# Routing of a mixture of experts: an own index test for the first gather, rows scaled by TensorE, slot weights moved into the first step

## The reference

```python
x = x + g1 * (jnp.concatenate([attn, rec], axis=-1) @ lp['w_out'])
h2 = modulate(rms_norm(x, lp['norm2']), sh2, sc2)
x = x + g2 * moe(h2, ...)
# moe: top-1 of 4 groups, then top-2 of the 8 experts in it
p_grp = softmax(x32 @ wg + bg); g_sel = argmax(p_grp)
top_v, top_i = lax.top_k(fine_sel, 2)
w_fine = softmax(top_v) * p_sel
act = silu(hg) * hu * combine;  y = einsum(act, w_down)
```

## Time and profile before

| | us |
|---|---|
| median of 3 runs | 623.18 (621.56 to 624.5) |
| the profiled execution's own time | 622.47 |
| its span, first to last instruction | 620.6 |
| TensorE busy | 584.6 (94%) |
| DVE / ACT / POOL busy | 350.2 / 179.7 / 101.7 |
| chain that ended last: TensorE / transfers / DVE | 73% / 15% / 5% |
| mean granted clock of TensorE | 0.991 |

### The profile page before, as it was taken

How to read it: one execution, slowest core, us unless ns; L and a number is a source line. 1 busy time by engine, 2 the same in 40 slices (tenths; PEclk the granted TensorE clock), 3 DMA queues, 4 the chain that set the end, 5 groups by cost and what they waited for, 6 DMA issues and landing times.

```text
span 620.6 us, 9361 instructions
## 1 busy us (share of the span) xinstructions
PE 584.6 (94%) x3274; PEld 325.4 (52%) x3275; DVE 350.2 (56%) x777; ACT 179.7 (29%) x375; POOL 101.7 (16%) x134
## 2 busy tenths in 40 slices
PE   5989999999998999999999889999999999987995
PEld 2544455555565677645555446555555555444542
DVE  2746898655565887654666883334342433341357
ACT  4203887701145777731111101111111111111110
POOL 4000011121261000000000111122212222221122
PEclk9999999999999999999999999999999999997998
DMA  8999833430039638539114959999999999999995
GB/s 320 378 370 361 337 124 147 175 136 2 0 85 270 265 101 265 236 126 383 68 69 143 379 175 384 420 419 417 419 417 416 417 420 420 421 417 418 412 403 224
DMA packets 48674, 176.21 MB, mean 284 GB/s; under 512 B 11540, under 2 KB 18592, under 8 KB 34944
## 3 DMA queue, kind: packets, MB, share of 16 engines
q1 hardware_dynamic: 36992, 154.86, 63.9%
q0 software_dynamic: 6688, 15.48, 7.2%
q10 hardware_dynamic: 4960, 5.42, 2.5%
HBM read 163.37 MB, written 21.14 MB: 297 GB/s over the span
## 4 chain that ended last, share of the span: by engine, by line
PE 73%; DMA 15%; DVE 5%; SPq 4%; issue 2%; ACTq 1%; DVEq 0%; ACT 0%; POOL 0%; POOLq 0%
PE ps L1802 18%; PE ps L1617 11%; PE ps L1542 8%; PE ps L1818 8%; PE ps L1530 7%; DMA expert_w<-exp_w_up 5%; PE ps L1657 4%; PE ps L1684 4%; DMA gate_w<-lru_wx 3%; PE ps L1666 3%; DMA w_mod_ring<-w_mod 2%; PE ps L1505 2%; SPq L369 2%; PE ps L1770 2%; PE ps L1451 2%; DMA recurrence<-w_mod 2%
## 5 line engine op out<-in xcount | busy, mean ns | idle before, releaser
L1802 PE MATMUL ps<-expert_w,hT_mixT 128*64 128x256 f32 x1120 | 135.6, 392 | 7.8 <-DMA expert_w<-exp_w_up 7.4
L1802 PEld LDWEIGHTS ps<-expert_w,hT_mixT 128*64 128x64 f32 x1120 | 84.5, 136 | 62.6 <-issue 19.1
L1530 PE MATMUL ps<-hT_mixT,w 128*128 128x128 f32 (+1 forms) x256 | 72.6, 437 | 1.2 <-DVE hT_mixT L954 1.2
L1617 PE MATMUL ps<-w,hT_mixT 128*128 128x512 f32 x160 | 71.9, 597 | 0.0
L1818 PE MATMUL ps<-expert_w,w 128*64 128x512 f32 x280 | 65.8, 598 | 0.0
L770 ACT ACTIVATE w<-ps 128x128 f32<-128x128 f32 x36 | 10.0, 277 | 188.4 <-PE ps L1802 188.4
L1530 PEld LDWEIGHTS ps<-hT_mixT,w 128*128 128x128 f32 x256 | 38.9, 191 | 35.8 <-issue 32.7
L1349 DVE SCALAR_TENSOR_TENSOR w<-w,ps 128x128 f32<-128x128 f32 x36 | 10.3, 287 | 81.2 <-ACT w L770 81.2
L1542 PE MATMUL ps<-w_qkv,hT_mixT 128*128 128x512 f32 (+1 forms) x160 | 53.1, 488 | 0.0
L1367 DVE TENSOR_TENSOR w<-ps,w 128x1024 f32<-128x1024 f32 x17 | 20.8, 1225 | 56.6 <-PE ps L1818 56.6
L1617 PEld LDWEIGHTS ps<-w,hT_mixT 128*128 128x128 f32 x160 | 29.1, 191 | 29.9 <-issue 29.7
(11 more groups left out here) (293 smaller groups left out, 759.5 us busy)
## 6 DMA issues: line engine op xcount, KB each, us to landing
expert_w<-exp_w_down SPq DMA_DIRECT2D x31, 1024.0 KB, 18.2
expert_w<-exp_w_gate SPq DMA_DIRECT2D x29, 1024.0 KB
expert_w<-exp_w_up SPq DMA_DIRECT2D x29, 1024.0 KB
w_mod_ring<-w_mod SPq DMA_DIRECT2D x14, 1024.0 KB, 6.5
y_rows<-zero_rows POOLq DMA_DIRECT2D x10, 512.0 KB, 9.4
expert_w<-y_rows SPq DMA_DIRECT2D x10, 512.0 KB, 9.8
recurrence<-w_mod SPq DMA_DIRECT2D x8, 512.0 KB, 9.7
w<-w_in SPq DMA_DIRECT2D x4, 1024.0 KB, 17.0
```

Source lines behind the costliest of these rows:

```text
L1530: ins = pe.matmul(ps[:, bank, 0:n], w1v[:, c, m * P:(m + 1) * P], HM[:, c, lo:lo + n], start=(c == 0), stop=(c == DC - 1))
L1617: ins = pe.matmul(ps[:, 2 * (t % 2) + half, :], HM[:, c, t * P:(t + 1) * P], w1v[:, c, half * 512:(half + 1) * 512], start=(c == 0), stop= ...
L1802: ins = pe.matmul(ps[r, 2 + k, 0:2 * P].rearrange("p (k f) -> p k f", k=2), xT[:, c, r], gate_up(i)[:, :, c, k:FF:FC], start=(c == 0), sto ...
```

## The change

Five things are done, all around the routing of the last tile.

1. **Index of the first gather.** In step 0 are the tokens of pair 0 in block 0. DVE makes `slots` of the last tile first, then `hit0` = (block number is 0) x (pair is 0), without the sums over pairs; ten matmuls with one column give the tokens, and DVE writes them into idxc, which the first gather uses. `hit`, its matmuls and `tid` follow.
2. **Rows of the last tile.** DVE doesn't make h2 of the last tile any more. ACT makes `diag`, the identity times the rows' factors, TensorE adds ident x shift2 and diag x scaled rows in banks 2 and 3, and ACT evicts them and writes them out.
3. **Logits of the last tile** are split: chunks 0 to 3 ahead of the last transposes.
4. **Slot weights.** The matmuls stand within the first expert step, behind its first half; `step1w` and `firsts` are made after `x_out(0)`.
5. **Smaller moves.** The g2 rows are issued after h2, the logits and `rank` of the last tile; the fillers are fewer and shorter; two semaphores of turns become one.

The names `fore` and `aft` are chunks 0 to 3 and 4 to 7.

```diff
+        hit0 = W1[:, 584:584 + TOP * NT // 2].bitcast(F16).rearrange("p (t k) -> p t k", t=NT)
...
+        diag = HM[:, 7, P:2 * P]
...
-            for i, v in enumerate((1, 0)):
-                sp.dma_start(g2[:, i, :], a["mod_rows"][v, 5 * D:6 * D].partition_broadcast(P)).then_inc(S["g2_in"], 16)
             sp.dma_start(kept_down[0], wd_v[KEPT, :, 0:D].rearrange("p (c n) -> p c n", c=DC)).then_inc(kept_in, 16)
             sp.wait_ge(S["h2"], NT)
             sp.wait_ge(S["lg_mm"], NT)
+            sp.wait_ge(S["rank_mm"], NT)
+            for i, v in enumerate((1, 0)):
+                sp.dma_start(g2[:, i, :], a["mod_rows"][v, 5 * D:6 * D].partition_broadcast(P)).then_inc(S["g2_in"], 16)
             sp.wait_ge(S["xg_in"], 16)
             sp.dma_start(ring[:, HOME[5], 0:EW], wg_v[5]).then_inc(wgu_in[2], 16)
             w_down(sp, 5, 5)
             sp.wait_ge(S["ssq2"], 2 * NT)
-            sp.wait_ge(S["idx_mm"], 1)
+            sp.wait_ge(S["idx_mm"], 2)
             sp.dma_start(kept_down[1], wd_v[KEPT, :, D:2 * D].rearrange("p (c n) -> p c n", c=DC)).then_inc(kept_in, 16)
             sp.wait_ge(S["route_ok"], 3)
...
+            act.wait_ge(S["rs2"], NT)
+            act.activation(diag, ident[:, :], ACT.Copy, scale=small[:, C_RS2 + NT - 1:C_RS2 + NT]).then_inc(S["diag"], 1)
+            for half in range(2):
+                act.wait_ge(S["h2_mm"], half + 1)
+                ins = act.activation(h2_last[:, 4 * half:4 * half + 4, :], ps[:, 2 + half, :].rearrange("p (c n) -> p c n", c=4), ACT.Copy)
+            ins.then_inc(S["h2"], 1)
             h2_out(NT - 1)
...
-            gather(tid[:, 0:1])
+            gather(idxc[:, 0:1])
+            pool.wait_ge(S["tid_ok"], 2)
             pool.wait_ge(S["xt_mm"], 1)
             gather(tid[:, 1:2])
...
             x1_out(last_tile)
-            h2(last_tile, slice(0, 4), False)
             choose(last_tile)
-            h2(last_tile, slice(4, DC), True)
             follow(last_tile)
             step(dve.memset(start[:, 0:1], 0.0))
 
-            dve.wait_ge(S["rank_mm"], NT)
+            slots(last_tile)
+            dve.scalar_tensor_tensor(out=hit0, in0=blockno, scalar=0.0, in1=ohp[:, :, :, 0], op0=ALU.is_equal, op1=ALU.mult)\
+               .then_inc(S["slot"], 1)
             step(dve.tensor_scalar(runs, ps[:, 7, 96:96 + NE], SLOTS / 2 - 0.5, 1.0 / SLOTS, ALU.add, ALU.mult))
             step(dve.tensor_scalar(runs, runs, ROUND, ROUND, ALU.add, ALU.subtract))
+            dve.wait_ge(S["idx_mm"], 1)
+            dve.tensor_scalar(idxc[:, :], ps[:, 4, 2 * COLS:2 * COLS + 1], float(TOK), None, ALU.add).then_inc(S["tid_ok"], 1)
             for q, (one, other) in zip((slice(0, PLAIN), slice(PLAIN, PAIRS)), members(runs)):
...
-            slots(last_tile)
...
 
-            dve.wait_ge(S["slot"], TOP * NT + 1)
+            dve.wait_ge(S["slot"], TOP * NT + 2)
...
-            dve.wait_ge(S["idx_mm"], 1)
+            dve.wait_ge(S["idx_mm"], 2)
             dve.tensor_scalar(tid[:, :], ps[:, 4, 0:COLS], float(TOK), None, ALU.add).then_inc(S["tid_ok"], 1)
...
-            dve.tensor_tensor(step1w, hit.rearrange("p t k n -> p (t k) n").unsqueeze(2).broadcast_to([P, TOP * NT, PARTS, COLS]),
-                              wparts.unsqueeze(3).broadcast_to([P, TOP * NT, PARTS, COLS]), ALU.mult).then_inc(S["stepw"], 1)
...
-            dve.tensor_tensor(firsts.rearrange("p t k n -> p (t k) n"), hit.rearrange("p t k n -> p (t k) n"),
-                              row_back.rearrange("p t k -> p (t k)").unsqueeze(2).broadcast_to([P, TOP * NT, COLS]), ALU.mult)\
-               .then_inc(S["stepw"], 1)
-            dve.wait_ge(S["tid_ok"], 1)
+            dve.wait_ge(S["tid_ok"], 2)
...
             x_out(0)
+            dve.tensor_tensor(step1w, hit.rearrange("p t k n -> p (t k) n").unsqueeze(2).broadcast_to([P, TOP * NT, PARTS, COLS]),
+                              wparts.unsqueeze(3).broadcast_to([P, TOP * NT, PARTS, COLS]), ALU.mult).then_inc(S["stepw"], 1)
+            dve.tensor_tensor(firsts.rearrange("p t k n -> p (t k) n"), hit.rearrange("p t k n -> p (t k) n"),
+                              row_back.rearrange("p t k -> p (t k)").unsqueeze(2).broadcast_to([P, TOP * NT, COLS]), ALU.mult)\
+               .then_inc(S["stepw"], 1)
             dve.wait_ge(S["w_mm"], 1)
...
+            dve.wait_ge(S["idx_mm"], 3)
...
+            def logits(t, chunks=range(DC)):
...
+                for c in chunks:
...
+                if chunks[-1] == DC - 1:
+                    ins.then_inc(S["lg_mm"], 1)
...
-            def keep_clock(count):
...
+                    pe.matmul(ps[:, 0, 0:n], ident[:, :], ring[:, HOME[0], 0:n], start=True, stop=True)
+
+            def last_rows_scaled():
+
+                pe.wait_ge(S["shift_in"], 32)
+                for half in range(2):
+                    cols = slice(half * 512, (half + 1) * 512)
+                    pe.matmul(ps[:, 2 + half, :], ident[:, :], shift2[:, cols], start=True, stop=False)
+                    if half == 0:
+                        pe.wait_ge(S["diag"], 1)
+                    pe.matmul(ps[:, 2 + half, :], diag, W1[:, 5 * D + half * 512:5 * D + (half + 1) * 512], start=False, stop=True)\
+                      .then_inc(S["h2_mm"], 1)
+
+            def slot_tokens(out, steps):
+
+                for t in range(NT):
+                    for k in range(TOP):
+                        ins = pe.matmul(out, slotp[:, t, k, :], steps[:, t, k, :],
+                                        start=(t == 0 and k == 0), stop=(t == NT - 1 and k == TOP - 1))
+                ins.then_inc(S["idx_mm"], 1)
+            pe.wait_ge(S["gated"], 2 * NT - 1)
+            pe.wait_ge(wgu_in[0], 64)
+            logits(NT - 1, fore)
+            keep_clock(1, 256)
             x1_turn(NT - 1, 1)
-            logits(NT - 1)
-            pe.wait_ge(S["gated"], 2 * NT - 2)
-            pe.wait_ge(wgu_in[0], 64)
-            keep_clock(4)
+            logits(NT - 1, aft)
+            last_rows_scaled()
+            keep_clock(1, 256)
             rank(NT - 1)
-            keep_clock(4)
+            keep_clock(1)
+            keep_clock(1, 256)
             pe.wait_ge(S["slot"], TOP * NT + 1)
-            for t in range(NT):
-                for k in range(TOP):
-                    ins = pe.matmul(ps[:, 4, 0:COLS], slotp[:, t, k, :], hit[:, t, k, :],
-                                    start=(t == 0 and k == 0), stop=(t == NT - 1 and k == TOP - 1))
-            ins.then_inc(S["idx_mm"], 1)
-            keep_clock(5)
+            slot_tokens(ps[:, 4, 2 * COLS:2 * COLS + 1], hit0.unsqueeze(3))
+            keep_clock(2)
+            pe.wait_ge(S["slot"], TOP * NT + 2)
+            slot_tokens(ps[:, 4, 0:COLS], hit)
+            keep_clock(3)
...
+            def slot_weights():
+
+                pe.wait_ge(S["stepw"], 1)
+                for t in range(NT):
+                    for k in range(TOP):
+                        ins = pe.matmul(ps[:, 4, P:P + PARTS * COLS], slot1[:, t, k, :],
...
+                ins.then_inc(S["w_mm"], 1)
+                pe.wait_ge(S["stepw"], 2)
+                for t in range(NT):
+                    for k in range(TOP):
+                        ins = pe.matmul(ps[:, 7, P:P + COLS], slot1[:, t, k, :], firsts[:, t, k, :],
...
+                ins.then_inc(S["idx_mm"], 1)
+
+            def step_of(n, s, visit, kept=False, routing=False):
...
                         ins.then_inc(S["gu_half"], 1)
+                        if routing:
+                            slot_weights()
...
             x_in(0)
-            pe.wait_ge(S["stepw"], 1)
...
+                visits(s, s, 1, routing=s == 0)
```

More of the change, by code:

```diff
@@ L246, in build @@
             "out_done v p act xg_in xt_mm gu_mm dn_mm xT_v xT_a th_ok act_ok aT_mm aT_ok y_v idxc_ok pidc_ok y_out "
-            "y_zero gu_half base stepw w_mm now gsel chosen tail_mm fin sg_ok pool_turn sp_turn cache_out st_col st_t st_ev").split()}
+            "y_zero gu_half base stepw w_mm now gsel chosen tail_mm fin sg_ok turn diag h2_mm cache_out st_col st_t st_ev").split()}
         rows_in = [sem(f"rows_in{i}") for i in range(NT)]
@@ L507, in _ @@
             sp.wait_ge(S["y_out"], 16 * end)
-            sp.sem_inc(S["sp_turn"], 1)
+            sp.sem_inc(S["turn"], 1)
             for t in range(NT):
@@ L854, in step_of @@
                 pool.wait_ge(S["xt_mm"], n + 2)
-                pool.sem_inc(S["pool_turn"], 1)
+                pool.sem_inc(S["turn"], 1)
                 gather(idxc[:, 0:1])
@@ L1333, in _ @@
             x_out(0)
-            dve.wait_ge(S["w_mm"], 1)
-            step(dve.tensor_copy(moved, ps[:, 5, 0:COLS]))
-            step(dve.tensor_tensor(info[:, :, 0], moved, ps[:, 5, COLS:2 * COLS], ALU.add))
-            step(dve.tensor_tensor(info[:, :, 0], info[:, :, 0], ps[:, 5, 2 * COLS:3 * COLS], ALU.add))
-            dve.wait_ge(S["idx_mm"], 2)
-            step(dve.tensor_scalar(moved, ps[:, 6, 0:COLS], float(TOK), None, ALU.add))
```

(44 more changed lines are left out.)

6 lines of the change are left out of this document (2 added, 4 removed).

## The result

The changed kernel took **624.71 us** (median of 20 runs, 622.09 to 628.03) against 622.69 for the kernel before (20 runs, 621.56 to 625.14, same chips): a ratio of 1.0033, 95% interval 1.0022 to 1.0045. That is within the 0.5% that I called the same, but it is a loss, and it lies outside my range of 618.9 to 623.5. The spread grew as well, and it goes with TensorE's clock: the ten runs whose mean granted clock was 0.987 or more have a median of 623.8, the ten at 0.984 or less one of 626.9. The profiled execution, 624.08 with a span of 622.3, had 0.991.

What follows compares the result with a forecast made beforehand. The end was taken to hang on the expert-weight stream, started by the first gather's landing. That landing 2.1 us sooner gave 622.47 − 2.1 = 620.4, or 621.1 against the median; range 618.9 to 623.5.

Steps and rivals of the forecast that it cites:

- the routing part: Last tile's routing: index ready at 360.0, rows written out at 357.0, first gather landing at 365.8, 2.1 us sooner.
- That term: Write of h2's last 128 rows, g2's first row sharing the queue: landing at 361.0, bounds 359.6 to 362.1.
- Rival 1: Write through before g2's packets start, in 2.6 to 3.2 us; gather lands 2.9 to 3.2 sooner: 620.1; chance 0.26.
- The base of 623.18: Median time of the kernel before, against which the 2.1 us gain was set to forecast 621.1.
- 367.93 less 364.8: Upper bound of the stream's gain, if indices bind and the first gather lands at 364.8: given as 3.2 us.
- so the first gate is done 0.5 us after TensorE asks. Left after step one: 0.6 to 0.9 us.: First expert step: DVE's first activation product 0.5 us late; of TensorE's 2.4 us earlier start, 0.6 to 0.9 remains.
- more is always queued than moves ... it resumes when the stream says: Expert steps: weight stream stays full from 367.97; TensorE, still waiting some 6 us, follows it; no new hole.
- rival 3: Clock falls in the routing stage, near 352; scaling takes 7.4 for 3.7 us: 624.6 to 627.7; chance 0.07.
- the longest idle stretch I work out is 1.2 us: Argument against a clock fall: TensorE idles at most 1.2 us, 367 to 368, where 1.48 now passes at full clock.
- Rival 2: Gain absorbed: write takes 5.1 us or rank comes late; stream starts only 0.5 to 1 us sooner: 622.4; chance 0.17.

Runs made afterwards that it cites:

- part 4 alone: Kernel before plus only slot matmuls inside the first expert step, with step1w and firsts after the first eviction: 624.92 us, ratio 1.0024.
- the pair at full clock: The one with all mends (0.9976), against it with DVE's g2 difference, counters and load late again and eight 128-column fillers in the stall: 623.41 us, 1.0000.
- the control: Changed kernel with only smallest and largest values given to its loads of loop bounds: 626.21 us, ratio 1.0058 to the kernel before.
- the one with all mends: Changed kernel with early DVE work, g2 after the write, four 512-column fillers, small fillers around last transposes and under the eviction: 621.60 us, ratio 0.9976.

## Why the prediction was wrong

**Right: the routing part.** `choose` started at 353.36 (I had 352.95), the index of the first gather was there at 360.32 (360.0), and the write went out at 357.50 (357.0). It landed after 4.43 us; I took 4.0, and the other kernels with g2 beside it show up to 5.9. That term was sized near the short end: the gather came 1.6 us sooner in the profiled run, not 2.1. That g2 beside the write lengthens it, as I assumed, is not shown (see the experiment with g2 behind it). The Trainium skill ("DMA: Bandwidth & Descriptors", section "Anatomy of one DMA") gives 2.0 us plus the bytes at 436 GB/s, from which an estimate for this write is 3.2 us. The section gives that for transfers that GpSimd issues, while ACT issues this one, so the rule was not meant for it; the runs show 2.6 to 5.9, on both sides. Rival 1 (the write lands alone) has no support in the change, and where it was brought about in one run, 2.6 us, the time stayed.

**Two slips in the sum.** The base of 623.18 was the median of three runs; twenty give 622.69, so the forecast from the right base would have been 620.6, and the miss is half a microsecond larger than it looks. And 367.93 less 364.8 is 3.1, not 3.2.

**Wrong, the step of the sum: "so the first gate is done 0.5 us after TensorE asks. Left after step one: 0.6 to 0.9 us."** The gate was 2.0 us late. The elements were named, five sums, the g2 difference and the row facts, but the 1.6 us of counters, load and loop entry between them was not, although the kernel before shows such a gap (1.21 us) in the same place. Before, that chain began at 369.81, before TensorE's step, and was hidden by it. Now it starts behind the slot matmuls at 372.88, 4.5 us into the step. With half clock, the first step ends 2.67 us late instead of 0.6 to 0.9 early.

**Wrong, the rule under it: "more is always queued than moves ... it resumes when the stream says".** The stream is full only as long as its requests come, and those are issued as TensorE uses up weights. 6 us of waiting at the end is no slack in the first step: 2.7 us there moved each refill that followed by as much (392.88 for 390.21, and still 478.59 for 475.92) and opened holes in 392 to 396 and at 478. The lead of 1.6 us went into them, as the sum of bytes shows. Three comparisons show the price: part 4 alone cost 0.24%, the pair at full clock differs by 0.24%, and taking the stall out at five fillers moved 1.0032 to 0.9989, with the fall of the clock behind it.

**Wrong in size: rival 3, the clock.** I gave it 0.07 and placed it in the routing stage, because "the longest idle stretch I work out is 1.2 us". There are three candidates, and I saw one: the stage at 352; the wait for the gather, where the last 512-column filler ends at 365.5 and the transposes begin 0.8 to 2.4 us behind it in the kernels with three fillers, with 0.85 for the eviction behind it; and the stall. In the profiled executions of the change and the twelve kernels here, the clock fell at the first place in three, at the second in six, at the third in two, and in the other two nowhere ahead of the waits for the last weights. I compared the fillers by number, 13 with 6, and never set their end beside the landing. Three fillers for five cost 0.19% alone, with an interval that only just leaves out nothing. The Trainium skill ("TensorE: Matmul & The Clock Gate", section "Why this matters for your kernels") names idle gaps between bursts as the danger. The traces agree at the second and third place, where the fall follows such gaps. At the first they don't tell: the change has the same gaps of 0.18 and 0.56 us there as two of the kernels with the fall, and no fall. The spread goes with the clock too, 623.8 or 626.9 by the mean of the run; at which place it fell in the longer runs is not known, as only one run of the change has a trace.

**Rival 2** ended at 622.4 by a shorter gain at the gather. The gain was absorbed, but by what comes behind it, which none of my cases had.

**In sum.** If all of it reached the end, the change would bring 1.6 us from the gather; the late gate costs 1.5, the lost fillers 1.2 (0.19% of 622.6), and other falls of the clock would be the remaining 0.9 of the measured 2.0; that last term is a difference, not a measurement, and the terms need not add. With the first two repaired and the idle stretches filled the same routing part gives 0.24% less than before.

**Open.** How much an earlier gather is worth at the end; why the clock falls at 352 to 356 in some executions and not in others; why the last packets of the write trail; whether the bounds on the loads cost time.

## What to carry to other kernels

- When work is moved behind a later wait, list everything that stands behind that wait on the same engine, with counters, loads and loop entries, and put ahead of it what doesn't need it: here that was worth more than the moved work.
- A stream whose refills are asked for by the consumer is full only while the consumer keeps its pace (254 and 238 GB/s for 410 and 426 here); waits for weights at the end don't make a delay at the start free.
- Fillers belong to the wait that they cover: write down when the last one ends and when the awaited transfer lands.

## What the hardware showed that I had not expected

- TensorE's clock went to 0.50 after a wait as short as 0.83 us with 0.85 us behind it (the control), and stayed full over 0.90 and 0.85 in the changed kernel's own trace, so these lengths alone don't decide it. One such fall costs 1.5 to 1.6 us in the first step (5.45 for 3.85).
- The same write of 512 KB took 2.6 to 5.9 us from its issue. With g2 issued 0.14 us behind it, g2's queue moved 0.39 MB between 361 and 362 in the changed kernel, and the write's queue two packets.
- The first gather held POOL for 1.18 us in the change, for 2.17 in the kernel with DVE's work early and five fillers, and for 2.49 in the one with all mends. Why is open.
